# Moving the weight splits, five page row sums and the head squares inside the attention jobs of a one-core decoder step

## What is computed

```
z = rmsnorm(x) @ w_in                  # q, k, v of 4 differential and 8 forgetting heads
q1, q2, ka_rot = rope(...)             # the differential group is rotated
a  = softmax(q1 k1^T) - lam * softmax(q2 k2^T);   oa = a @ v      # causal, 128-row blocks
of = softmax(qf kf^T + C[t] - C[s]) @ vf                          # causal
# sample tokens: the same against 8 pages of 128 cached rows each, fetched by a page table
x  = x + rmsnorm(concat(rmsnorm(oa), of) @ w_o)
x  = x + rmsnorm((gelu(conv3(h @ w_gate)) * (h @ w_up)) @ w_down)
```

## Time and profile before

| | us |
|---|---|
| median of 3 runs (lowest, highest) | 1506.2 (1505.4, 1510.13) |
| the profiled execution, its own time | 1511.48 |
| its span in the profile | 1509.7 |
| TensorE busy in it | 1442.5 (96%) |
| VectorE, ScalarE, GpSimd busy | 862.5, 636.9, 370.2 |
| attention stage, from and to | about 150 to 675 |

### The profile page before, as it was taken

The page is one execution under the profiler, slowest core; times in us unless marked ns, Lnnn a source line. Parts: engine busy times, 40 slices in busy tenths (PEclk is TensorE's granted clock), DMA queues, the critical chain, the costliest instruction groups (busy, mean ns, idle before and its releaser), DMA issues. The chain is left out here.

```text
span 1509.7 us, 26823 instructions
## 1 busy us (share of the span) xinstructions
PE 1442.5 (96%) x10396; PEld 1297.5 (86%) x10396; DVE 862.5 (57%) x1378; ACT 636.9 (42%) x1194; POOL 370.2 (25%) x548
## 2 busy tenths in 40 slices
PE   7999989999998999889999999999999999999998
PEld 6999777767767677468789999999999999999998
DVE  6412566565554546465547876666776646444673
ACT  6723555544354434443332633323333324343543
POOL 5213876764654442032100000000000000000120
PEclk9999999999999999899999999999999999999999
DMA  5213546666755654622223222222222236655773
GB/s 183 56 35 92 176 153 220 213 209 227 240 174 181 199 181 124 202 85 71 71 84 93 71 77 79 85 84 85 71 85 71 71 133 207 202 187 178 235 263 112
DMA packets 174840, 209.91 MB, mean 139 GB/s; under 512 B 22051, under 2 KB 118891, under 8 KB 174676
## 3 DMA queue, kind: packets, MB, share of 16 engines
q1 hardware_dynamic: 174714, 208.21, 43.6%
HBM read 178.37 MB, written 29.88 MB: 138 GB/s over the span
## 5 line engine op out<-in xcount | busy, mean ns | idle before, releaser
L629 POOL TENSOR_TENSOR k_page<-k_page,q_bc 128x256 f32<-128x256 f32 x256 | 186.9, 762 | 130.3 <-DMA k_page<-in_cache_fox_k 102.8
L1205 PE MATMUL PS<-ht_hi,w_hi 128*128 128x344 f32 x576 | 196.5, 341 | 6.3 <-POOL w_lo L600 3.3
L1205 PE MATMUL PS<-ht_hi,w_lo 128*128 128x344 f32 x576 | 186.8, 324 | 0.0
L1205 PE MATMUL PS<-ht_lo,w_hi 128*128 128x344 f32 x576 | 186.7, 324 | 0.0
L2435 PE MATMUL PS<-act_hi,wd_hi 128*128 128x344 f32 x528 | 169.2, 321 | 2.6 <-DVE act_lo L2270 2.6
L2435 PE MATMUL PS<-act_hi,wd_lo 128*128 128x344 f32 x528 | 168.8, 320 | 0.0
L2435 PE MATMUL PS<-act_lo,wd_hi 128*128 128x344 f32 x528 | 168.6, 319 | 0.0
L838 ACT ACTIVATE probs<-probs,stat 128x256 f32<-128x256 f32 (+7 forms) x128 | 98.7, 772 | 137.6 <-DVE stat L1082 137.3
L2267 DVE TENSOR_TENSOR wd_lo<-wd_raw,wd_hi 128x1024 fp32r<-128x1024 f32 (+1 forms) x88 | 85.8, 978 | 112.2 <-ACT act_hi L2078 92.3
L1205 PEld LDWEIGHTS PS<-ht_hi,w_hi 128*128 128x128 f32 x576 | 111.3, 193 | 32.1 <-issue 25.1
L2075 ACT ACTIVATE wd_hi<-wd_raw 128x1024 fp32r<-128x1024 f32 (+1 forms) x88 | 74.2, 844 | 139.1 <-DMA act_raw<-a_dram 102.5
(11 more groups left out here) (280 smaller groups left out, 3319.5 us busy)
## 6 DMA issues: line engine op xcount, KB each, us to landing
wd_raw<-in_w_down SPq DMA_DIRECT2D x44, 512.0 KB, 3.5
k_page<-in_cache_diff_k SPq DMA_DIRECT2D x64, 256.0 KB, 2.9
k_page<-in_cache_fox_k SPq DMA_DIRECT2D x64, 256.0 KB, 3.1
v_page<-in_cache_diff_v SPq DMA_DIRECT2D x64, 256.0 KB, 2.8
v_page<-in_cache_fox_v SPq DMA_DIRECT2D x64, 256.0 KB, 3.1
w_raw<-in_w_in SPq DMA_DIRECT2D x24, 512.0 KB, 4.6
a_dram<-conv SPq DMA_DIRECT2D x22, 516.0 KB, 3.1
act_raw<-a_dram SPq DMA_DIRECT2D x66, 172.0 KB, 3.7
```

Of the source, the lines that this page charges most:

```text
L629: ins = pool.tensor_tensor(kpage[:, g % 2, c:c + PIECE], kpage[:, g % 2, c:c + PIECE], qbc[:, c:c + PIECE], ALU.mult)
L1205: ins = pe.matmul(PS[0:rows, z_bank(c), 0:THIRD], b[:, k, :], a[:, k, third(i)], start=(k == 0 and p == 0), stop=(k == KC - 1 and p == 2))
```

## The change

It moves instructions and changes none. The numbers of instructions and DMAs are the same.

- Splits: the key tile for the unit after next is split in the job t = 6 and no longer t = 5. Within a job ACT splits after the exponentials, and POOL after its pages, rotations and head factors.
- Rotations (`rope` on POOL): in the jobs up to 3 they come ahead of the pages.
- Five key pages, the second of a doubled job (g = 10, 19, 28, 37, 46; page 55 is excepted, since it is the last of its batch), are summed on DVE two jobs later, behind `weights`, and no longer at the end of the next job.
- Head squares: one job later, behind the exponentials, with POOL's factor in the same job as before.

```
+    second_page = lambda g: g > EARLY_PAGES and k_job(g) == k_job(g - 1) and g % PAGES < PAGES - 1
@@ POOL, for J in range(NJ):
-                n = {1: k_tile(u + 1) + 1, 5: k_tile(u + 2)}.get(t, len(TILES))
-                if n < len(TILES):
-                    split_lo(n)
+                ropes = [c for c, h in fill(J - 1)[0] + fill(J - 1)[1] if h] if J else []
+                if J <= ROPE_FIRST:
+                    for c in ropes:
+                        rope(c)
                 for g in k_pages(J):
                     if g % PAGES == PAGES - 1:
                         later_pages(g // PAGES)
                     multiply(g)
-                if J:
-                    for c, h in fill(J - 1)[0] + fill(J - 1)[1]:
-                        if h:
-                            rope(c)
+                if J > ROPE_FIRST:
+                    for c in ropes:
+                        rope(c)
...
+                n = {1: k_tile(u + 1) + 1, 6: k_tile(u + 2)}.get(t, len(TILES))
+                if n < len(TILES):
+                    split_lo(n)
@@ ACT, for J in range(NJ + 2):
-                n = k_tile(u + 1) + 1
-                if t == 1 and n < len(TILES):
-                    split_hi(n)
                 if J >= 2:
                     turned(J - 2)
...
                 if J < NJ:
                     exponentials(J)
+                for v in range(NT):
+                    if norm_job(v) + 1 == J:
+                        if v == 0:
+                            act.wait_ge(norm_sems["zeroed"], 1)
+                        head_squares(v)
+                n = {1: k_tile(u + 1) + 1, 6: k_tile(u + 2)}.get(t, len(TILES))
+                if n < len(TILES):
+                    split_hi(n)
...
-                for v in range(NT):
-                    if norm_job(v) == J:
-                        if v == 0:
-                            act.wait_ge(norm_sems["zeroed"], 1)
-                        head_squares(v)
...
-                n = k_tile(u + 2)
-                if t == 5 and n < len(TILES):
-                    split_hi(n)
@@ DVE, for J in range(NJ + 3):
                 if 1 <= J <= NJ:
                     weights(J - 1)
+                for g in k_pages(J - 2):
+                    if second_page(g):
+                        reduce_page(g)
...
                 for g in range(2, EARLY_PAGES) if J == 0 else k_pages(J - 1):
-                    reduce_page(g)
+                    if not second_page(g):
+                        reduce_page(g)
```

More of the change, by code:

```diff
@@ L288, in project @@
     LAST_UNIT = NJ - NT
+    ROPE_FIRST = 3
     FT = 4
```

## The result

The changed kernel takes 1520.5 us (median of 8 runs, 1516.1 to 1523.0), the kernel before 1508.2 us beside it (8 runs). The ratio is 1.0075, with a 95% interval of 1.0058 to 1.0091: slower by about 11.3 us. The forecast was +10.9 us, and 1517 us on the median of 1506.2 that was known then.

The account below looks back on a forecast made before the run. TensorE, busy 96% of the span, bounds the kernel; only its holes can be won. Chunk delays 13.2 + clock 4.0 - copies 8.9 - clock 1.7 + new waits 4.3 = +10.9 us: 1517 on the median, range 1504 to 1525.

Parts of the forecast that it names:

- The key tile's split behind the page: PE's first key tile chunks wait for POOL's split behind the page: units 1 to 3 +4.0, +1.9, +4.2 us.
- Unit 0, +1.2 forecast: Key tile split behind page 11, started at 201.27, ends after the chunk's old start: +1.2 us; value tiles' splits cost nothing.
- The page sum: Second page's sum moved on DVE: PE's waits for weights mostly go, by itself worth most of 9.1 us, plus clock.
- the rival in which page and split come in time: Pages land some 6 us earlier, PE finds its split ready: -20 us, 1486; chance 0.12 including a half case at 1505.
- Turned copies, -8.9: Ten PE waits for ACT's copies a_t behind squares or splits all go: -8.9 us.
- New waits on ACT's copies, +4.3: Squares and splits at their new place delay ACT's copies in jobs 38, 53, 36: +4.3 us; other five places have slack.
- Head norms beside POOL, +1.9: Unit 4: DVE's four head norms run beside POOL's split, 3.00 us for 1.13; unit costs +1.9 us, not +0.4.
- the +2.8 worked out from the rule: Unit 4: by the shared-port rule each of four norms could wait for a 0.7 us split instruction: +2.8 us.
- The clock, +4.0 - 1.7 = +2.3: Slow clock behind new holes of units 1 and 3, 2.0 us each; the slow stretch behind 467.3 goes, -1.7.
- that the holes hurt less: Rival: no clock lost behind new holes (-4.0), moved copies find slack (-4.3): +2.6 us, 1509; chance 0.16.
- That the lateness travels: Rival: late split delays POOL's next page, loads and value tile; more clock lost: 1523 to 1525 us; chance 0.14.

Follow-up runs that it names:

- kernel 1: Changed kernel with POOL's lower half of the key tile's split ahead of that job's key page, not behind it: 1494.9 us, ratio 0.9909.
- kernel 10: Changed kernel with SP's load of only the first of the two key pages of jobs t = 6 ahead of the value pages: 1502.9 us.
- Kernel 5: Kernel before with only the value tile's split (job t = 1) and the rotations of jobs 1 to 3 moved: 1506.4 us, ratio 0.9979.
- kernel 3: Kernel before with only the row sums of a doubled job's second key page moved two jobs later on DVE: 1502.2 us, ratio 0.9953.
- kernel 4: Kernel before with only the head squares moved one job later, behind the exponentials: 1507.4 us, ratio 0.9986.
- Kernel 8: Changed kernel with POOL's key split ahead of its page, plus squares, head factor and head norms moved earlier: 1491.2 us, ratio 0.9873.
- kernels 2 and 6: 2: kernel before with only the key tile's split moved, 1530.4 us; 6: changed kernel with both key pages' loads ahead of value pages, 1532.8 us.
- kernel 9: Changed kernel with POOL's key split ahead of its page, rows_out ahead of the moved page sum, and head work early: 1487.7 us.

## Why the prediction was right

The sum of +10.9 us met the measured +11.3 (interval 8.7 to 13.7), and its main steps were right: the split waits behind the page, SP and the DMA hold the page, the old waits go and new ones come. That it met the number within half a microsecond is in part luck, since terms were off by 1 to 3 us and made up for one another. The first chunk of each key tile against the one before gives the terms unit by unit. Each forecast is made of the terms of the sum that fall between two of these chunks (the slow clock behind a hole at a first chunk falls into the next stretch), the measured one of the earlier trace rows and the timeline above (22: 545.78 against 531.56; end of the stage 680.0 against 667.5). The measured time is split into PE's holes and its busy time; the matmuls are the same, so a change in busy time is one of the clock.

| stretch | forecast holes | forecast clock | measured holes | measured busy | forecast, measured us |
|---|---|---|---|---|---|
| to key tile 12 | +1.2 | 0 | +2.1 | +1.8 | +1.2, +3.9 |
| 12 to 14 | 4.0 - 0.6 = +3.4 | 0 | +3.4 | +0.4 | +3.4, +3.8 |
| 14 to 16 | 1.9 - 0.6 = +1.3 | +2.0 | +0.8 | +1.2 | +3.3, +2.0 |
| 16 to 18 | +4.2 | 0 | +3.9 | +1.2 | +4.2, +5.0 |
| 18 to 20 | 1.9 + 1.7 + 1.0 - 1.8 = +2.8 | +2.0 | +1.4 | +2.5 | +4.8, +3.8 |
| 20 to 22 | -4.6 | -1.7 | -1.1 | -3.3 | -6.3, -4.4 |
| 22 to the end | -1.3 + 1.6 = +0.3 | 0 | +0.1 | -1.9 | +0.3, -1.7 |
| sum | +8.6 | +2.3 | +10.5 | +1.9 | +10.9, +12.5 |

- **The key tile's split behind the page.** Right in mechanism and near in size, and shown by kernels 1 and 2: four holes of 3.0 to 4.7 us for `w_lo`, the split starting where page 20 ends, DMA and SP's order ahead of the page (kernel 10). DVE and ACT didn't matter (kernel 1 has their moves and not the loss). One reading was off: POOL stood idle for 3.8 to 5.2 us ahead of three of these pages, but only for 2.0 us ahead of page 11.
- **Unit 0, +1.2 forecast, +3.9 measured.** I took the start of page 11, 201.27, as given, and the splits of the value tiles as costing nothing. Both were wrong. The page started 2.5 us later (203.81 by POOL's timeline), since POOL's pages are a chain here: a second rotation, of 3.1 us, now stands ahead of page 6 (before, one rotation and the value tile's split did), and the page starts at 175.34 in place of 172.0. The value tile's split, now behind page 5 and the first rotation, ends at 172.3 (166.4 before), and PE's chunk of job 3 waits for it until 172.36, where it began at 172.72 before. The 6.8 us behind this hole of 1.96 us ran at 0.75, those behind the old one of 2.72 us at 1.00, which is most of the 1.8 us of busy time. Kernel 5, with this part alone, has the same delay at page 6 and the same hole for the split (2.15 us). These rows are of the changed kernel:

```profile
169.53 2.78 POOL L602 TENSOR_TENSOR w_lo<-w_raw,w_hi 128x256 fp32r<-128x256 f32 x4
172.26 0.93 POOL L651 TENSOR_TENSOR z_raw<-z_raw,cos 128x344 f32<-128x344 f32 x1
...
175.34 2.80 POOL L631 TENSOR_TENSOR k_page<-k_page,q_bc 128x256 f32<-128x256 f32 x4
...
189.19 1.99 POOL L631 TENSOR_TENSOR k_page<-k_page,q_bc 128x256 f32<-128x256 f32 x2 [4.06 <-DMA q_bc<-qs_dram]
...
203.81 3.36 POOL L631 TENSOR_TENSOR k_page<-k_page,q_bc 128x256 f32<-128x256 f32 x4 [2.90 <-DMA k_page<-in_cache_fox_k]
```

- **The page sum.** The waits for weights fell as forecast. But in the rival in which page and split come in time I had counted 9.1 us of holes and 4.6 of clock for it; kernel 3 gave 4.5 us of holes and 1.4 of clock up to tile 20, nothing behind it, and 7.1 us in all by its median. The moved sum left waits of its own, four of 0.73 us. Kernel 1, which comes close to that rival, took 1495 us and not 1486.
- **Turned copies, -8.9.** The waits for `a_t` fell by 9.3 us, and all ten holes of the list are gone, so the count was right; not all of it reached the end. From tile 20 to 22 I forecast -4.6 us of holes and -1.7 of clock; measured were -1.1 and -3.3. The hole of 2.07 us ahead of tile 22, which I had left as it was, is 4.89 us now. It ends 17.7 to 18.5 us after SP's issue of the value pages ahead of page 56, in the kernels before and after and in kernel 4, so what PE gains on that way, here 1.7 us of clock above all, it waits for at the unit's end. Kernel 8 shows it from the other side: with the norms moved forward the chain takes 14.5 us and the hole is 1.69 us.
- **New waits on ACT's copies, +4.3.** Measured 1.66 us (job 38), 1.40 (job 53) and 1.46 for the copy of key rows (job 36): 4.5 us. But I had given the other five places slack, and job 46 had none. There squares and split stand together ahead of the copy, as in job 38:

```profile
529.31 0.85 PE L1329 MATMUL PS<-ident,probs 128*128 128x128 f32 x6 [1.39 <-ACT o_transposed L898]
```

  With it the new waits are 5.9 us.
- **Head norms beside POOL, +1.9.** The norms of unit 4 took 2.58 us where they took 1.13, +1.5; the row was nearer than the +2.8 worked out from the rule. The hole behind them grew by only 0.6 us (2.10 to 2.73). In unit 5 they were beside POOL before already.
- **The clock, +4.0 - 1.7 = +2.3.** PE's busy time for the stage rose by 1.5 to 1.9 us, depending on where the window ends. Near, but as a sum of errors. The stretches behind the new holes of the units 1 and 3 had 0.62 and 0.60: (1 - 0.62) x 6.8 = 2.6 and 2.7 us where I assumed 2.0 each. Unit 0 cost 1.8 us that I had not counted, and from tile 20 on 5.2 us came back where I had counted 1.7. For the last 1.9 of these no part of the change gives a reason.

The rivals: that the holes hurt less fell, since the clock behind them cost more than I had assumed and the copies found no slack. That the lateness travels needed +17 us; the measured 11.3 are short of that, though in unit 0 it did travel, from page 6 to page 11. Set against kernel 1, in which the split is in time, holes of 16.3 us in all cost 24 us of the stage: in these two executions each microsecond of hole came with almost half a microsecond of slow clock. A comparison with the kernel before hides this in part, since that kernel had lost clock behind other holes in the units 0 and 2.

## What to carry to other kernels

When an instruction is moved behind another one on the same engine, its new time is that of the other's last input: ask which queue issues that input and what stands ahead of it there, before asking how long the instruction itself takes. A change in several parts should be measured in parts: here one of four lost 20 us and hid that another gained 7 us, and putting back four instructions per unit turned +0.75% into -0.9%. And count a hole by what follows it too, and by halves of a stage: kernel 3 had the same sum of holes as the kernel before, because it won 5.9 us where its edit stands and PE's next long wait took back what the clock gave later on.

## What the runs showed of the hardware

- Four head norms on DVE take 1.13 us while POOL is idle and 2.57 to 3.00 us beside POOL's multiplications or splits. One then lasts up to 0.82 us; in the 3.00 us case they start 0.73 us apart ((3.00 - 0.81) / 3), which is POOL's pace beside them: 2.92 us for four instructions, in place of 2.77. The Trainium skill, "SBUF — State Buffer", section "SBUF: two separate sides", says that a DVE operation with two SBUF inputs and a GpSimd one share a pair of ports, and that the one that starts first keeps it until its instruction ends. The trace agrees in that DVE keeps to POOL's pace of 0.73 us; that POOL loses only 0.15 us over four turns does not look like a full exchange of turns, and no run here shows why.
- The stage's mean granted clock ranged from 0.94 (kernels 2 and 6) to 0.99 (kernel 9) for the same matmuls; PE's busy time followed from 475.7 to 455.7 us. Between the profiled executions of the kernels 2 and 9 the clock is worth 20 us, the holes 26 (60.3 and 34.4 us). The length of a hole alone does not tell the clock of the next 6.8 us: behind 2.72 us (before) it was 1.00, behind 1.96 us (changed) 0.75; behind 3.02, 4.19, 4.73 and 4.89 us (changed) 0.73, 0.60, 0.62 and 0.78; behind a pair of 0.17 and 0.73 us (kernel 3) 1.00, behind pairs of 0.75 and 0.73 us (kernel 1, unit 1) and 0.73 and 0.73 us (kernel 3, unit 0) 0.75, and behind 0.73 and 0.73 us in unit 0 of kernel 1 again 1.00.
- A load's landing time depends on what is in flight: the 256 KB of page 20's last part took 2.7 us in kernel 10, where it was issued ahead of the value pages, and 4.4 us in the changed kernel behind them. `q_bc` (512 KB) took 5.8 us in kernel 4, and a 4 KB load issued behind it 4.8 us, where such a load takes 3.0 us in the median.
